# Decoder block with 32 streamed experts: raw weight chunks retired early, and the first gather cut in two

## What is computed

```
logits = hf @ w_router + b_router
top_v, top_i = top_k(logits, 4);  gate = softmax(top_v)
for each expert e, on the tokens that chose it:
    gu  = xb @ w_gu[e] + b_gu[e]                    # 1024 -> 2048
    g   = min(gu[:, :1024], 7);  u = clip(gu[:, 1024:], -7, 7)
    act = g * sigmoid(1.702 * g) * (u + 1)
    y  += gate * (act @ w_down[e] + b_down[e])      # 1024 -> 1024
```

## Time and profile before

| what | us |
|---|---|
| median of 3 runs (lowest, highest) | 1238.45 (1238.29, 1239.51) |
| the profiled execution | 1239.43 |
| its span in the trace | 1237.7 |
| PE busy in the span | 1179.7 (95%) |
| DVE, ACT, POOL busy | 307.4, 230.3, 230.1 |
| all 192 pairs of expert weights | 403 MB of the 450.00 MB read |

### The profile page before, as it was taken

How to read it: one execution, slowest core, us unless ns; L and a number is a source line. 1 busy time by engine, 2 the same in 40 slices (tenths; PEclk the granted TensorE clock), 3 DMA queues, 4 the chain that set the end, 5 groups by cost and what they waited for, 6 DMA issues and landing times.

```text
span 1237.7 us, 13553 instructions
## 1 busy us (share of the span) xinstructions
PE 1179.7 (95%) x5931; PEld 579.5 (47%) x5931; DVE 307.4 (25%) x463; ACT 230.3 (19%) x312; POOL 230.1 (19%) x200
## 2 busy tenths in 40 slices
PE   9999999999999999999999999998999999898996
PEld 9987788988433333333333333333333333333332
DVE  5447364224411212121122112111211211121112
ACT  6473676445100000000000000000000000000001
POOL 6977759982000000000000000000000000000000
PEclk9999999999999999999999999999999999999999
DMA  9644437648999999999999999999999999999994
GB/s 315 206 136 136 170 103 244 247 164 346 406 412 415 426 429 427 427 428 428 428 428 427 428 427 429 426 428 427 427 427 428 428 429 428 426 428 428 428 427 191
DMA packets 54120, 451.99 MB, mean 365 GB/s; under 512 B 6668, under 2 KB 6760, under 8 KB 29352
## 3 DMA queue, kind: packets, MB, share of 16 engines
q1 hardware_dynamic: 54056, 451.06, 88.6%
HBM read 450.00 MB, written 1.05 MB: 364 GB/s over the span
## 4 chain that ended last, share of the span: by engine, by line
PE 62%; DMA 33%; DVE 3%; ACT 1%; issue 1%; POOL 0%; DVEq 0%; ACTq 0%; POOLq 0%
PE ps L1155 21%; DMA ring<-in_w_down 18%; PE ps L1177 11%; PE ps L778 10%; DMA spare<-in_w_down 7%; DMA kv_small<-in_w_down 7%; PE ps L723 6%; PE ps L1133 4%; PE ps L1101 2%; PE ps L1085 2%; PE ps L1197 1%; PE ps L744 1%; PE ps L802 0%; PE ps L762 0%; PE ps L890 0%
## 5 line engine op out<-in xcount | busy, mean ns | idle before, releaser
L467 POOL TENSOR_TENSOR w_parts<-ring,w_parts 128x512 fp32r<-128x512 f32 x162 | 219.3, 1389 | 45.9 <-ACT w_parts L1326 41.8
L616 POOL TENSOR_SCALAR ss<-ss 128x2 f32<-128x2 f32 (+2 forms) x7 | 1.3, 192 | 955.2 <-ACT junk L1316 950.9
L1155 PE MATMUL ps<-ring,xs 128*64 128x512 f32 x640 | 143.9, 596 | 10.5 <-DMA ring<-in_w_gu 9.7
L1994 DVE TENSOR_SCALAR xbuf<-ps 128x512 f32<-128x512 f32 x32 | 22.1, 691 | 525.1 <-PE ps L1155 525.1
L1155 PE MATMUL ps<-ring,nT 128*64 128x512 f32 x608 | 136.6, 595 | 8.7 <-DMA ring<-in_w_gu 8.7
L1177 PE MATMUL ps<-ring,xbuf 128*64 128x512 f32 x592 | 134.2, 597 | 7.4 <-DMA ring<-in_w_down 7.4
L778 PE MATMUL ps<-w_parts,xT_hi 128*128 128x512 f32 x352 | 112.1, 399 | 0.0
L1564 ACT ACTIVATE xbuf<-xbuf 128x512 f32<-128x512 f32 x32 | 20.2, 631 | 461.8 <-DVE xbuf L1994 461.8
L1155 PEld LDWEIGHTS ps<-ring,xs 128*64 128x64 f32 x640 | 43.9, 137 | 101.6 <-issue 80.9
L1326 ACT ACTIVATE w_parts<-ring 128x2048 fp32r<-128x2048 f32 x41 | 78.3, 1917 | 68.1 <-PE ps L778 42.4
L1574 ACT ACTIVATE xbuf<-ps 128x512 f32<-128x512 f32 x32 | 19.2, 599 | 371.2 <-PE ps L1197 371.2
(11 more groups left out here) (292 smaller groups left out, 1247.3 us busy)
## 6 DMA issues: line engine op xcount, KB each, us to landing
ring<-in_w_gu SPq DMA_DIRECT2D x78, 2048.0 KB, 43.2
ring<-in_w_down SPq DMA_DIRECT2D x36, 2048.0 KB, 42.8
kv_small<-in_w_gu SPq DMA_DIRECT2D x13, 2048.0 KB, 39.3
gates_xn<-in_w_gu SPq DMA_DIRECT2D x13, 2048.0 KB, 44.3
ring<-in_w_in SPq DMA_DIRECT2D x24, 1024.0 KB, 5.4
spare<-in_w_gu SPq DMA_DIRECT2D x12, 2048.0 KB, 43.7
xcq<-in_w_gu SPq DMA_DIRECT2D x11, 2048.0 KB, 44.6
xcq<-in_w_down SPq DMA_DIRECT2D x8, 2048.0 KB, 38.8
```

The source lines that it names most:

```text
L467: ops.tensor_tensor(w_lo[:, m % SPLIT, c], ring_slot(m)[:, c], w_hi[:, m % SPLIT, c], ALU.subtract).then_inc(lo_ready[name], 1)
L1155: i = mm(ps[64 * half:64 * half + 64, 4 + q, :], xg[:, k, (j % GE) * SLOTS:(j % GE + 1) * SLOTS], w[:, q * FF + half * 512:q * FF + half * ...
L1994: V.tensor_scalar(gl, ps[:, 4, :], LIM, None, ALU.min).then_inc(gl_ready, 1)
```

## The change

1. **Raw slots and halves.** Chunks 35 to 41 get slots and halves by a table: slots 0, 1, 4, 0, 1, 4 and X_SLOT; halves 0, 1, 0, 1, 0, 1 from 36 on. Ring slots 2 and 3 and the third buffer of halves are thereby done with some chunks earlier. Two pairs of expert 0 are fetched among the raw chunks: pair 0 behind chunk 37, pair 1 behind chunk 39. PAIR_ORDER is new. ACT's `splits_to` calls are placed anew: chunk 38 after high_tiles (2, 3), 40 after the exponentials, 41 after the copies of o.
2. **Group 0 in halves.** `half_gather(k0, e0, bank)` gathers for two experts (128 columns). Experts 0 and 1 are gathered around expert 0 as before; experts 2 and 3 during expert 1, in four `rest_gather` calls: after its first chunk, before down, after down, and after combine. DVE takes each with `take_half`. `turn_first` comes after the third chunk of expert 1 and not the second, and turns the hot rows first. The next group's one-hot is made after the last take.
3. **The end of the experts.** down(30) writes bank 4, and turn_act of expert 31 stands in its middle (into `actT_last`); combine of 30 and turn_hot of 31 stand in the middle of down(31).
4. **Output.** DVE scales and SP writes in four pieces of 512 columns and not two of 1024.

The core of the diff:

```
+LATE_SLOT = {35: 0, 36: 1, 37: 4, 38: 0, 39: 1, 40: 4, 41: X_SLOT}
+LATE_HALF = {36: 0, 37: 1, 38: 0, 39: 1, 40: 0, 41: 1}
 def slot(m):
-    return m % RING_SPLIT
+    return LATE_SLOT.get(m, m % RING_SPLIT)
+def half_of(m):
+    return LATE_HALF.get(m, m % SPLIT)
+def last_in(place, m):
+    return max((i for i in range(m) if place(i) == place(m)), default=None)
...
-PAIR_ORDER = [1, X_SLOT // 2, KV_SMALL, halves_pair(FRONT_CH - 3), 0, GATES_XN,
-              halves_pair(FRONT_CH - 2), halves_pair(FRONT_CH - 1)]
+PAIR_ORDER = [1, halves_pair(2), 0, KV_SMALL, GATES_XN, halves_pair(0), X_SLOT // 2, halves_pair(1)]
+EARLY_PAIRS = {37: 0, 39: 1}
+FIRST_G = 2 * GU_PR
...
+                if slot(m) == X_SLOT:
+                    sp_.wait_ge(chunk_used, products_done(FIRST["xq"]))
+                elif last_in(slot, m) is not None:
+                    for eng, count in lo_counts(last_in(slot, m)).items():
                         sp_.wait_ge(lo_ready[eng], count)
...
+                if m in EARLY_PAIRS:
+                    q = EARLY_PAIRS[m]
+                    first_free(q)
+                    fetch_gate_up(pair_home(q), 0, gu_at(0, q), pair_full[q])
...
+            def half_gather(k0, e0, bank):
+                w = 2 * SLOTS
+                for k in range(2):
+                    for b in range(TB):
+                        i = mm(ps[:, bank, k * w:(k + 1) * w], hn2[:, b, (k0 + k) * P:(k0 + k + 1) * P],
+                               onehot[:, b, e0:e0 + 2, :].rearrange("p e s -> p (e s)"), start=(b == 0), stop=(b == 1))
+                i.then_inc(gathered, 1)
+            def rest_gather(k0):
+                if k0:
+                    pe.wait_ge(gather_out, GU_PR + k0 // 2)
+                half_gather(k0, 2, 7)
...
-                gather(k0, 7 - k0 // 2 % 2)
+                half_gather(k0, 0, 7 - k0 // 2 % 2)
...
-                    if between is not None and k == 3:
+                    if between is not None and k == 1:
+                        rest_gather(0)
+                    if between is not None and k == 5:
                         between()
...
             def turn_first():
-                pe.wait_ge(act_ready, 1)
-                turn_act()
                 pe.wait_ge(gt_out, 1)
                 pe.wait_ge(rk_ready, 1)
                 turn_hot(0)
+                pe.wait_ge(act_ready, 1)
+                pe.wait_ge(gather_out, GU_PR + 1)
+                turn_act()
...
+                if n == 1:
+                    rest_gather(2)
                 pe.wait_ge(ht_out, n)
                 down(lambda c, n=n: main_home(dn_at(n - 1, c)))
+                if n == 1:
+                    rest_gather(4)
...
                 combine()
-                if n in (2, 3):
-                    pe.wait_ge(gather_out, 2 * n + 1)
+                if n == 1:
+                    rest_gather(6)
+                    turn_hot(n)
+                    pe.wait_ge(gather_out, FIRST_G)
...
+            pe.wait_ge(at_out, NE - 1)
+            pe.wait_ge(ht_out, NE - 1)
+            pe.wait_ge(gu_read, NE)
+            down(lambda c: main_home(dn_at(NE - 2, c)), bank=4, between=turn_last_act)
+            pe.wait_ge(at_out, NE)
+            down(lambda c: main_home(dn_at(NE - 1, c)), tail=True, acts=actT_last, between=combine_last_but_one)
             pe.wait_ge(ht_out, NE)
-            pe.wait_ge(at_out, NE)
-            down(lambda c: main_home(dn_at(NE - 1, c)), tail=True)
...
-                    if m >= SPLIT:
-                        act.wait_ge(chunk_used, m - SPLIT + 1)
+                    if last_in(half_of, m) is not None:
+                        act.wait_ge(chunk_used, last_in(half_of, m) + 1)
...
             high_tiles(TR_H1, xT_hi, g_xattn_k, (0, 1), h_hi)
-            splits_to(38)
             act.wait_ge(stripe_out["dve"], emptied(FIRST["out"] + 1)[1])
             squares(h[:, 0, :], 8)
             high_tiles(TR_H1, xT_hi, g_xattn_k, (2, 3), h_hi)
             splits_to(39)
             n = FIRST["xq"]
-            splits_to(products_done(n) + SPLIT - 2)
...
-            empty(FIRST["xv"])
+            splits_to(40)
+            empty(FIRST["xv"], splits=False)
...
+            splits_to(41)
...
+                for half in range(2):
+                    c = slice(half * SW, (half + 1) * SW)
+                    V.scalar_tensor_tensor(out=xn[:, b, c], in0=whole[b][:, c], scalar=ss[:, 12 + b:13 + b],
+                                           in1=gfin[:, c], op0=ALU.mult, op1=ALU.mult).then_inc(out_ready, 1)
```

More of the change, by code:

```diff
@@ L410, in build @@
             sem, ("x_in", "prm_in", "dtw_in", "mem_in", "late_in", "moe_in", "gf_in"))
-        slot_full = [sem(f"slot_full{i}") for i in range(RING_SPLIT)]
+        slot_full = [sem(f"slot_full{i}") for i in range(X_SLOT + 1)]
         pair_full = [sem(f"pair_full{i}") for i in range(PAIRS)]
@@ L702, in pairs @@
             def pairs(m, src):
-                hi, lo = (w[:, m % SPLIT, :].rearrange("p (k n) -> p k n", k=4) for w in (w_hi, w_lo))
+                hi, lo = (w[:, half_of(m), :].rearrange("p (k n) -> p k n", k=4) for w in (w_hi, w_lo))
                 return [(hi, src[0]), (lo, src[0]), (hi, src[1])]
@@ L1162, in gate_up, with down @@
                         first_gather(k + 3)
-                    if between is not None and k == 3:
+                    if between is not None and k == 1:
+                        rest_gather(0)
+                    if between is not None and k == 5:
                         between()
-            def down(homes, tail=False):
+            def down(homes, tail=False, bank=6, acts=actT, between=None):
                 for k in range(FF // P):
@@ L1181, in down, with turn_hot @@
                         i.then_inc(chunk_used, 1)
+                    if between is not None and k == 3:
+                        between()
             def main_home(m):
                 return main_full(m), pair_filled(m), main_pair(m)
-            def turn_hot(j):
+            def turn_hot(j, bank=6):
                 for b in range(TB):
-                    i = nc.tensor.transpose(ps[:, 6, b * P:(b + 1) * P],
+                    i = nc.tensor.transpose(ps[:, bank, b * P:(b + 1) * P],
                                             gatehot[:, b, j % GE].rearrange("p u s -> p (u s)"), ident[:])
@@ L1239, in _, with turn_last_act, combine_last_but_one @@
                 combine()
-                if n in (2, 3):
-                    pe.wait_ge(gather_out, 2 * n + 1)
+                if n == 1:
+                    rest_gather(6)
+                    turn_hot(n)
+                    pe.wait_ge(gather_out, FIRST_G)
+                elif n in (2, 3):
+                    pe.wait_ge(gather_out, FIRST_G + 2 * n - 3)
                     gather(GATHERED_IN[n][1])
                     turn_hot(n)
-                    pe.wait_ge(gather_out, 2 * n + 2)
+                    pe.wait_ge(gather_out, FIRST_G + 2 * n - 2)
                 elif 4 <= n < NE - 1:
-                    pe.wait_ge(gather_out, n + GE + 1)
+                    pe.wait_ge(gather_out, n + FIRST_G + 1)
                 pe.wait_ge(act_ready, n + 1)
                 turn_act()
-                if n not in (2, 3):
+                if n > 3:
                     turn_hot(n)
+            def turn_last_act():
+                pe.wait_ge(act_ready, NE)
+                turn_act()
+            def combine_last_but_one():
+                pe.wait_ge(yb_ready, NE)
+                combine()
+                turn_hot(NE - 1, 5)
+            pe.wait_ge(at_out, NE - 1)
[4 more added lines that the diff above has]
+            down(lambda c: main_home(dn_at(NE - 1, c)), tail=True, acts=actT_last, between=combine_last_but_one)
             pe.wait_ge(ht_out, NE)
-            pe.wait_ge(at_out, NE)
-            down(lambda c: main_home(dn_at(NE - 1, c)), tail=True)
             def overflow_experts(it):
@@ L1332, in normalise, with empty @@
                 af(dst[:, 0], src[:, 0], ACT.Copy, scale=ss[:, c0:c0 + 1]).then_inc(normed_act, 1)
-            def empty(n, func=ACT.Copy, scale=1.0, ahead=True):
+            def empty(n, func=ACT.Copy, scale=1.0, ahead=True, splits=True):
                 name, _, _, _, layout, _ = STRIPES[n]
                 b0, i = 2 * (n % 2), n - FIRST[name]
-                splits_to(products_done(n) + SPLIT - 2)
+                if splits:
+                    splits_to(products_done(n) + SPLIT - 2)
                 act.wait_ge(chunk_used, products_done(n))
-                if ahead:
+                if ahead and splits:
                     splits_to(products_done(n) + SPLIT - 1)
@@ L2062, in _ @@
                 dve.wait_ge(rstd, 6 + b)
-                V.scalar_tensor_tensor(out=xn[:, b, :], in0=whole[b], scalar=ss[:, 12 + b:13 + b], in1=gfin,
-                                       op0=ALU.mult, op1=ALU.mult).then_inc(out_ready, 1)
+                for half in range(2):
+                    c = slice(half * SW, (half + 1) * SW)
```

(2 more changed lines are left out.)

122 lines of the change are left out of this document (70 added, 52 removed).

## The result

| | before | changed |
|---|---|---|
| median us (8 runs each) | 1238.48 | 1241.76 |
| lowest to highest | 1237.95 to 1239.51 | 1240.10 to 1247.59 |
| ratio (95% interval) | | 1.003 (1.0022 to 1.0039) |
| profiled execution, its span | 1239.43, 1237.7 | 1240.10, 1238.3 |

What follows compares the result with a forecast made beforehand. The stream of w_down pairs over the DMA was taken to set the end. Terms of +1.1 (stream), -0.9 (tail) and -0.4 (output) summed to -0.2 us, so a median of 1238.3, own range 1236.6 to 1240, widened with rivals to 1235.8 to 1240.8.

Steps and rivals of the forecast that it cites:

- What bounds the kernel: Whole kernel: the last pair's landing sets the end; PE's lateness matters only where it makes a hole in the stream.
- Early pairs give nothing: First filling: its last pair lands at about 322.5, but the next waits for chunk 0's release; a 4 us hole.
- Stall in chunk 38: Front, second xq chunk: PE waits 1.3 us for POOL's low tiles, and the front ends 1.3 us later.
- Start of expert 0: Before expert 0: DVE's half take saves 0.27 us; the gathers' shortening saves nothing, since DVE comes later.
- Half gather and expert 2: Experts 0 and 1: a half gather costs 1.05 us; six halves replace two whole ones, +2.66 us before expert 2.
- Slack at chunk 11: Chunk 11's release: 3.7 us later, less 2.6 of slack, moves its landing and the last one by +1.1 us.
- Tail: End of the kernel: down(31) ends 0.9 us sooner, and the output in quarters saves 0.4 us.
- sign of being wrong: Profile after: no stall at chunk 38, or a stream that isn't empty at chunk 11's release.
- the filling pays a little: Rival, chance 0.21: no stall in chunk 38 and half gathers of 0.9 us; 1236.0 us in all.
- the filling does all it could: Rival, chance 0.03: early filling takes two pairs off the stream, -9.8 us, 1227.
- half gathers cost like whole ones: Rival, chance 0.10: 1.7 us each, 3.9 more on PE before chunk 11, wholly a hole; 1242.2 us.
- more stalls in the front: Rival, chance 0.11: two buffers of halves also stall chunk 41 or 40 by 1.3 us each; 1239.6 to 1241.

Runs made afterwards that it cites:

- e11: The changed kernel with the edits of e7 and e8 together; 1238.61 us, ratio 1.0004 to the kernel before.
- e8: The changed kernel with ACT making chunk 38's high half before high_tiles (2, 3), not behind; 1239.93 us, ratio 1.0009 to the kernel before.
- e7: The changed kernel with the second half gather's matmuls done three times, keeping PE busy before expert 0; 1240.29 us.
- e4: The changed kernel itself, run again beside the follow-up kernels; 1241.48 us.
- e1: The kernel before with only the new end of the experts and the output in quarters; 1238.21 us, ratio 0.9997.
- e10: The changed kernel with the gathers for k0 = 0 and 2 whole and chunk 38's split before high_tiles (2, 3); 1237.44 us, ratio 0.9992 to the kernel before.
- e2: The kernel before with only the late slots, two buffers of halves and two early pairs; 1239.98 us, ratio 1.0009.
- e3: The kernel before with only group 0 gathered in halves; 1240.54 us, ratio 1.0014.
- e6: The kernel before with 32 unneeded transposes once behind combine in expert 1; 1239.62 us, ratio 1.0012.
- e5: The kernel before with 16 unneeded transposes once behind combine in expert 1; 1239.09 us, ratio 1.0003.

## Why the prediction was wrong, step by step

- **What bounds the kernel**: right. The stream of pairs is full from the changed kernel's 380 us on, and the landings set the end. Among the profiles of the changed kernel and its mends, the span follows chunk 11's release nearly one to one: 373.80 and 1236.9 (e11), 373.91 and 1237.0 (e8), 375.57 and 1238.3 (changed), 376.90 and 1239.9 (e7), 378.83 and 1241.6 (e4). With the same end but chunk 11 within its slack it no longer does: 370.78 and 1236.1 (e1), 371.54 and 1235.3 (e10).
- **Early pairs give nothing**: right, by the hole at 320 to 325 and by e2 and e10.
- **Stall in chunk 38**: right in place and cause, 1.67 instead of 1.3; e8 took it away. Chunks 40 and 41 brought no further one.
- **Start of expert 0, "the gathers' own shortening saves nothing here"**: right for the take, and wrong in what it left out. The shortening makes PE's wait for DVE 2.12 instead of 0.72, and I gave this idle time no price. After it the clock fell to 0.50 in e4's trace, and the chunk behind it took 5.35 and not 3.65. This is the step that failed. e7, which fills the wait and changes nothing else, gets 1.2 us back, and the same edit on top of e8 1.3. Of all executions, 11 of 41 of the kernels with this wait (the changed one twice, e3, e8) have a mean granted clock of 0.996 or less, one of 100 of the others, and none of the 103 of the kernel before beside them. The mean doesn't say where the clock fell: the one of the 100 is e6's profiled execution, whose falls lie elsewhere, and the changed kernel's 1247.59 at 0.946 lost far more than one chunk can.
- **Half gather and expert 2**: 1.09 for 1.05, and from expert 0 to expert 2 it is 3.35 more and not 2.66. Of the difference 0.15 are the six half gathers (five at 1.09 and one at 1.00). Another 0.26 are the turns ahead of expert 2: they are 0.46 longer, 0.30 of it the wait for the last take, where I had put 0.2. The rest, 0.3, are expert 1's chunks beside half gathers, one of which takes 3.59 from start to start and not 3.49.
- **Slack at chunk 11**: 2.6, which e5 and e6 allow and don't fix. The lateness that it met was not 3.7 but 4.8: 375.57 - 371.81, plus the 1.00 by which this execution's front happened to be early. So the term was +2.2, not +1.1: the slack was right, and the lateness ahead of it 1.1 too small.
- **Tail**: -0.9 was -0.6 in the trace, 0.4 of it was lost at the last combine, and -0.4 for the output came: together -0.6 and not -1.3, as in e1's trace.

The sum as measured: 4.8 - 2.6 - 0.6 = +1.6 with a full clock, where the executions at 0.999 show 1.7 (1240.07, 1238.35). The clock's 1.2 (e7) makes it 2.8, of the 2.9 to 3.3 in the two series; what is left, 0.1 to 0.5, isn't settled. Against the forecast of 1238.3 the stream's 1.1 and the tail's 0.7 alone give 1240.1, inside the range; with the clock it is 1241.3, outside. Neither sign of being wrong that the prediction named came about, and none of them looked at the clock. The rivals: "the filling pays a little" and "the filling does all it could" fell (the holes), "half gathers cost like whole ones" too (1.09), and "more stalls in the front" as well (30.97 for 30.95). The slower side came about, but through a mechanism that wasn't among them. The Trainium skill, "TensorE: Matmul & The Clock Gate", section "LDWEIGHTS (loading the stationary operand)", makes a half gather 0.86 as an estimate, and the trace has 1.09. It agrees for products in a row: the second eight ahead of expert 0 take 0.89 (2.05 - 1.16), so that 0.2 are the change of tile shape.

One point was only argued: that the clock fell in expert 0 in the longer executions of these kernels. It is shown there in one trace; for the others there are the mean clock and what e7 and e11 gain by filling the wait.

## What to carry to other kernels

A buffer filled earlier is worth nothing if the next one waits for work that hasn't moved; look for the first recycled buffer, not the first free one. Slack is spent once: price a lateness where it meets the stream, and add up everything ahead of that place before taking the slack off. Ask too what it is slack against: a lateness that moves all releases alike (e2) uses none of it and goes through. Before you shorten TensorE's work ahead of a wait that another engine ends, ask what the idle time does to its clock: here it was cheaper to leave PE busy. And compare series, not one profile with one profile.

## What was not expected of the hardware

- The granted clock fell from 1.00 to 0.50 and back in the middle of the work, in some executions and not in others. At expert 0 of e4 PE had done 2.05 us of half gathers and then waited 2.13; with PE busy over the same stretch (e7: 3.84 of gathers, 0.34 of waiting) the first chunk took 3.65 at a clock of 1.00. At 830 us of e6 the work ahead of the wait of 2.13 was two full chunks of 3.65 and a gather. The products of ones, behind 128x32 products, took 4.10 to 4.11 with no wait ahead of them in three of the fourteen profiles (e6, which has whole gathers, and e4 and e7, which have halves) and 2.48 in the others.
- A transfer that was issued when its queue was about to run empty cost more than the prediction's 7.7 and 4.9 say: in the changed kernel the pair issued at about 327.4 took 9.8 us to land, 6.5 after the one ahead of it and not 4.9, with 393 and 364 GB/s in the windows from 325 and 330. The same transfer took 9.1 in e4 and e8, 1.3 to 1.4 later than the two numbers give, and 8.8 in e10.
